# A two-layer hybrid encoder on one core: reciprocal roots computed as exp(−½·ln) on ScalarE

## The chip, the cores and the metric

The kernel runs on one core of a Trainium2 chip, as one launch. The metric is the time of one execution on the device, in microseconds; the profile adds the span, from the first to the last instruction of a profiled execution. A core has TensorE (PE), VectorE (DVE), ScalarE (ACT), GpSimd (POOL) and SyncE (SP), each with its own in-order queue of instructions, and 16 DMA engines.

## The reference, cut to what matters

256 tokens of 1024 features pass two layers, all in f32. A layer mixes tokens in three branches, sums them through an output projection, and then adds a feed-forward part (PEER) that gathers rows from two tables of experts, chosen by scores. Seven places of a layer divide by a root:

```
h  = x * rsqrt(mean(x*x) + 1e-6)                     # input norm
q, k = q * rsqrt(mean(q*q) + 1e-6), k * ...          # attention, 16 norms per token
o  = o * rsqrt(mean(o*o) + 1e-6)                     # attention output, per head
out = out * rsqrt(mean(out*out) + 1e-6)              # state-space branch
kk = kk / max(sqrt(sum(kk*kk)), 1e-12)               # RWKV branch, per head
y  = (y - mean) * rsqrt(var + 64e-5)                 # RWKV branch, output norm
f  = x * rsqrt(mean(x*x) + 1e-6)                     # input of the feed-forward part
```

The feed-forward part takes 128 experts per token (8 heads of 16): it gathers a row of table u for each, multiplies it with the token's normed features, applies a gelu, weighs it, gathers the expert's row of table v, and sums those rows by weight.

## The kernel before, in words

The work is cut in four units of 128 tokens: layer 0 with tokens 0 to 127 and 128 to 255, then layer 1 with the same. A unit has a mixing (the three branches and the output projection), a choosing of experts (`peer`, `chosen`), and a gather of 256 rows of 128 x 1024 f32, 128 of table u and 128 of table v. POOL issues one indirect DMA per row (L614) into a ring of 15 buffers (`arena`). A row of table u is multiplied with the features on DVE (L1804, L1806); a row of table v is added either on PE (L2393, L2394), by a diagonal matrix of the weights that ACT writes (L1038, four rows ahead, eight diagonals in a ring), or on DVE (L1813, L1817). A buffer is free for the next row once DVE or PE is done with it, and POOL waits for that.

The mixing of unit 0 runs by itself, before there is any expert to gather. From then on the gather of unit n and the mixing and choosing of unit n+1 run beside each other. Every engine has them in one fixed order: the table `ROWS_BY` says, for each named step of the next unit, how many rows of the present one come before it. An engine that waits in a step therefore also holds back the rows that stand behind the step in its queue. The last unit's gather has no mixing beside it.

Each root is taken in the same way: PE or DVE sums the squares, ACT takes the root with the scale and the small constant built in (`x_length` L800, `kk_length` L722, `qk_lengths` L728, `s5_root` L753, `o_roots` L795, `deviation` L857, and in `peer` L993), and DVE inverts it (L1387, L1340 and L1341, L1434, L1284, L1376, L1532, L1698) and multiplies. ACT goes on only when its own result is written. In unit 0 (`first`) the order is written out by hand; in later units the steps `scale`, `gelu`, `abkr`, `saa`, `vara` and `fT` hold them.

ACT evaluates its functions from a table that holds a set of them. Nothing in the kernel's source loads a table: the loads (ACT_TABLE_LOAD in the profile) are put in when the program is built, each in front of an instruction whose function the loaded set lacks. The profile names the line of that instruction, not the set. Copy and Square never have one in front of them here. In `first` three small instructions are there to have a table loaded early: a Sqrt (L862), a Tanh (L878) and an Exp (L882), each on one column.

Of the kernel before, what the change touches and what calls it, by code (L numbers as in the profile page):

```python
# [18 lines left out]
ALU = mybir.AluOpType  # L19
# [3 lines left out]
P = 128  # L23
D_MODEL = 1024
# [179 lines left out]
def build_program(nc, A, out):  # L204
    ctx = ExitStack()
    with ctx:  # L206
        def sb(name, shape, dt=F32):
            return ctx.enter_context(nc.sbuf_tensor(name, shape, dt))
# [47 lines left out]
        small = sb("small", [P, 64])  # L256
        eps = sb("eps", [P, 2])
        cum = sb("cum", [P, 2, P + 1])
# [153 lines left out]

        f_sd, f_r, f_g, f_h, fT_ps, fT_a, fT_v = (sem(i) for i in ("f_sd", "f_r", "f_g", "f_h", "fT_ps", "fT_a", "fT_v"))
        x_half = sem("x_half")
# [161 lines left out]
        def _(pool):  # L576
            own = Chain(s_pool, pool)

            own.add(nc.gpsimd.memset(eps[:, 0:1], NORM_EPS))
            own.add(nc.gpsimd.memset(eps[:, 1:2], RW_EPS))  # L580
            own.add(nc.gpsimd.iota(ti[:], pattern=[[1, P]], base=0, channel_multiplier=0))
            pool.wait_ge(s_pool, own.count)
# [38 lines left out]
        def _(act):  # L621
# [53 lines left out]
            def mixing(n, layer, t):  # L675
# [43 lines left out]
                def kk_length():  # L719

                    act.wait_ge(lora_ps, n + 1)
                    A_(rw["rk"][:, :, :], quad(3)[:, 2:4, :], ACT.Sqrt).then_inc(kk_sd, 1)  # L722
                    act.wait_ge(kk_sd, n + 1)

                def qk_lengths():

                    act.wait_ge(qk_ss, n + 1)
                    A_(small_m[:, 32:48], small_m[:, 16:32], ACT.Sqrt, bias=eps[:, 0:1], scale=1.0 / HD).then_inc(qk_sd, 1)  # L728
                    act.wait_ge(qk_sd, n + 1)
# [20 lines left out]
                def s5_root():  # L750

                    act.wait_ge(gss_ps, n + 1)
                    A_(glu_t[:, 0, :], bank[s5b][:, 0:P], ACT.Sqrt, bias=eps[:, 0:1], scale=1.0 / 256).then_inc(gss_sd, 1)  # L753
                    act.wait_ge(gss_sd, n + 1)
# [37 lines left out]
                def o_roots():  # L792

                    act.wait_ge(oss_ps, n + 1)
                    A_(normed[:, n % 2, 512:1024], bank[4][:, :], ACT.Sqrt, bias=eps[:, 0:1], scale=1.0 / P).then_inc(oss_sd, 1)  # L795
                    act.wait_ge(oss_sd, n + 1)

                def x_length():

                    A_(small_m[:, 1:2], small_m[:, 0:1], ACT.Sqrt, bias=eps[:, 0:1], scale=1.0 / D_MODEL).then_inc(x_sd, 1)  # L800
                    act.wait_ge(x_sd, n + 1)
# [52 lines left out]
                def deviation():  # L854

                    act.wait_ge(var_ps, n + 1)
                    A_(rw["ep"][:, :, :], quad(1)[:, 0:2, :], ACT.Sqrt, bias=eps[:, 1:2], scale=1.0 / HD).then_inc(var_sd, 1)  # L857
                    act.wait_ge(var_sd, n + 1)

                def first():  # L860

                    own(A_(small_a[:, 30:31], eps[:, 0:1], ACT.Sqrt))  # L862
                    act.wait_ge(st_ss, 1)
# [110 lines left out]
            def peer(n, layer, t):  # L974
# [17 lines left out]
                own(A_(work[:, 0:D_MODEL], x[:, t, :], ACT.Square, accum_out=small_p[:, 0:1]))  # L992
                A_(small_p[:, 1:2], small_p[:, 0:1], ACT.Sqrt, bias=eps[:, 0:1], scale=1.0 / D_MODEL).then_inc(f_sd, 1)  # L993
                act.wait_ge(f_sd, n + 1)
# [4 lines left out]
                for g, heads in enumerate(TOP):  # L999
                    yield f"s{g}"  # L1000
                    chunk_used(act, n, Q_NAMES[heads[-1] | 1 if n else heads[-1]])
                    b0 = 2 * heads[0] % 4
                    A_(q_cm[:, 2 * heads[0]:2 * heads[-1] + 2, :], bank_all[:, b0:b0 + 2 * len(heads), 0:P] if n else quad(g % 2)[:, 0:2 * len(heads), :],
                       ACT.Copy).then_inc(pq_ok, 1)
                    act.wait_ge(pq_ok, NT * n + g + 1)
                    act.wait_ge(ps_ps, NT * n + g + 1)
                    if g == 0:
                        act.wait_ge(f_r, n + 1)
                    A_(scores[:, 2 * heads[0]:2 * heads[-1] + 2, :], score_bank(n, g)[:, 0:2 * len(heads), :], ACT.Copy,
                       scale=small_p[:, 2:3]).then_inc(ps_ok, 1)  # L1010
                    act.wait_ge(ps_ok, NT * n + g + 1)
                    if n == 0 and g == 0:
                        normed_copied(0)
# [54 lines left out]
        def _(dve):  # L1068
# [139 lines left out]
            def mixing(n, layer, t):  # L1208
# [72 lines left out]
                def s5_normed():  # L1281

                    dve.wait_ge(gss_sd, n + 1)
                    own(V.reciprocal(glu_t[:, 0, :], glu_t[:, 0, :]))  # L1284
                    for hf in range(2):
# [51 lines left out]
                def products():  # L1337

                    dve.wait_ge(kk_sd, n + 1)
                    own(ts(rw["rk"][:, :, :], rw["rk"][:, :, :], 1e-12, None, ALU.max))  # L1340
                    own(V.reciprocal(rw["rk"][:, :, :], rw["rk"][:, :, :]))  # L1341
                    own(tt(rw["kk"][:, :, :], rw["kk"][:, :, :], rw["rk"][:, :, :], ALU.mult))
                    dve.wait_ge(exps, n + 1)
# [28 lines left out]

                def o_scale():

                    dve.wait_ge(oss_sd, n + 1)
                    own(V.reciprocal(normed[:, n % 2, 512:1024], normed[:, n % 2, 512:1024]))  # L1376

                def attended():

                    stt(mixed[:, 0:4, :].rearrange("p a t -> p (a t)"), bank[3][:, :], subln[:, layer:layer + 1],  # L1380
                        normed[:, n % 2, 512:1024], ALU.mult, ALU.mult).then_inc(mix_d, 1)
                    dve.wait_ge(mix_d, n + 1)

                def scaled():

                    dve.wait_ge(x_sd, n + 1)
                    own(V.reciprocal(small_m[:, 2:3], small_m[:, 1:2]))  # L1387
                    ts(normed[:, n % 2, :], x[:, t, :], small_m[:, 2:3], None, ALU.mult).then_inc(h_ok, 1)
                    dve.wait_ge(h_ok, n + 1)
# [41 lines left out]
                def qk_normed():  # L1431

                    dve.wait_ge(qk_sd, n + 1)
                    own(V.reciprocal(small_m[:, 32:48], small_m[:, 32:48]))  # L1434
                    for i in range(2):
# [93 lines left out]
                def gated():  # L1529

                    dve.wait_ge(var_sd, n + 1)
                    own(V.reciprocal(rw["ep"][:, :, :], rw["ep"][:, :, :]))  # L1532
                    own(tt(rw["y"][:, :, :], rw["y"][:, :, :], rw["ep"][:, :, :], ALU.mult))
# [7 lines left out]
                def first():  # L1541
# [49 lines left out]
                    right_side()  # L1591
                    o_scale()
                    attended()
# [7 lines left out]
                def beside_rows():  # L1601
# [57 lines left out]
                    yield "y"  # L1659
                    o_scale()  # L1660
                    attended()
# [30 lines left out]
            def peer(n, layer, t):  # L1692
# [4 lines left out]
                dve.wait_ge(f_sd, n + 1)  # L1697
                V.reciprocal(small_p[:, 2:3], small_p[:, 1:2]).then_inc(f_r, 1)  # L1698
                dve.wait_ge(f_r, n + 1)
                ts(normed[:, n % 2, :], normed[:, n % 2, :], small_p[:, 2:3], None, ALU.mult).then_inc(f_h, 1)  # L1700
# [734 lines left out]
```

## Time and profile before

| | |
|---|---|
| time, median of three runs | 1849.23 us (1845.07 to 1852.96) |
| profiled execution, span | 1836.8 us |
| profiled execution, own time outside the span | not recorded |
| DVE busy | 1418.5 us, 77% |
| ACT busy | 383.6 us, 21% |
| POOL busy | 1133.0 us, 62% |
| PE busy | 1366.3 us, 74% |
| HBM traffic | 638.65 MB read, 348 GB/s over the span |
| ACT_TABLE_LOAD | 73, of 1283 ns each |

An engine's busy time is an average over stages with different limits. In the rows below a timeline row begins with the start and the duration in us; the bracket at its end is the idle time of the engine just ahead of it and what ended that. "issue" means that the profile shows nothing that it waited for. A DMA share near 1 says that all 16 DMA engines are busy.

### The profile page before, as it was taken

Reading aid. Unit: us, or ns where it says so; the run is one execution under the profiler, and the core shown is the slowest. Engines: PE = TensorE matmul, PEld = TensorE weight load, DVE = VectorE, ACT = ScalarE, POOL = GpSimd, SP = SyncE. Lnnn points to the kernel's source line nnn. Section 1 sums busy time; section 2 is a strip of 40 time slices with the busy share of each in tenths; the row PEclk is TensorE's granted clock in tenths of the full one; section 3 lists DMA queues with packets and bytes.
Section 4 is the critical chain, followed back from the end, with each engine's and each line's share of the span. In section 5 each row is a group of like instructions: output and inputs, shape, how many; then the busy total and the mean of one; then the engine's idle time right before and its main releaser. Section 6 shows DMA issues by size and latency. Waiting matters only on the chain. (4 is left out here: it accounts for less than half of the span.)

```text
span 1836.8 us, 17575 instructions
## 1 busy us (share of the span) xinstructions
PE 1366.3 (74%) x5274; PEld 783.4 (43%) x5274; DVE 1418.5 (77%) x3427; ACT 383.6 (21%) x933; POOL 1133.0 (62%) x1046
## 2 busy tenths in 40 slices
PE   7889498687978388867888777967978837555557
PEld 6567354255456144334455363434546413222122
DVE  7867699997679669898668799887867875576653
ACT  2332221322111121322121221311221212001000
POOL 2002576777674756477657787576677766666664
PEclk9979699989899689989899989988999958978989
DMA  7348998999999998998999999999999999999998
GB/s 222 127 146 285 337 367 336 409 367 357 373 401 395 331 371 310 338 352 321 387 386 404 403 393 407 338 346 346 364 381 405 386 392 348 357 354 354 371 367 323
DMA packets 204723, 640.90 MB, mean 349 GB/s; under 512 B 18603, under 2 KB 35861, under 8 KB 204629
## 3 DMA queue, kind: packets, MB, share of 16 engines
q0 software_dynamic: 147920, 538.25, 77.0%
q1 hardware_dynamic: 56172, 100.96, 15.6%
q8 instruction: 43, 0.70, 0.2%
q10 hardware_dynamic: 536, 0.57, 0.1%
q14 instruction: 52, 0.42, 0.1%
HBM read 638.65 MB, written 1.05 MB: 348 GB/s over the span
## 5 line engine op out<-in xcount | busy, mean ns | idle before, releaser
L614 POOL DMA_INDIRECT arena<-in_peer_u_dram,expert x512 | 563.6, 1101 | 416.8 <-DVE expert L1768 150.3
L614 POOL DMA_INDIRECT arena<-in_peer_v_dram,expert x512 | 559.7, 1093 | 264.8 <-issue 152.4
L2393 PE MATMUL bank<-arena,diag 128*128 128x512 f32 x768 | 443.1, 660 | 269.2 <-DMA arena<-in_peer_v_dram,expert 122.2
L1806 DVE SCALAR_TENSOR_TENSOR arena<-arena,normed 128x1024 f32<-128x1024 f32 x364 | 434.1, 1224 | 70.5 <-DMA arena<-in_peer_u_dram,expert 53.7
L2394 PE MATMUL bank<-arena,diag 128*128 128x512 f32 x768 | 426.6, 637 | 7.3 <-issue 6.9
L2393 PEld LDWEIGHTS bank<-arena,diag 128*128 128x128 f32 x768 | 141.0, 205 | 474.4 <-issue 408.2
L2394 PEld LDWEIGHTS bank<-arena,diag 128*128 128x128 f32 x768 | 158.3, 206 | 213.9 <-issue 213.9
L1804 DVE SCALAR_TENSOR_TENSOR arena<-arena,bank 128x1024 f32<-128x1024 f32 x148 | 175.7, 1219 | 77.5 <-DMA arena<-in_peer_u_dram,expert 46.5
L1038 ACT ACTIVATE diag<-ident,weight 128x128 f32<-128x128 f32 x384 | 128.6, 391 | 235.6 <-DVE weight L1823 101.2
L1881 PE MATMUL bank<-h_cm,wring 128*128 128x128 f32 x1152 | 150.0, 291 | 32.0 <-issue 20.2
L1881 PEld LDWEIGHTS bank<-h_cm,wring 128*128 128x128 f32 x1152 | 146.1, 207 | 45.6 <-issue 37.5
L1817 DVE SCALAR_TENSOR_TENSOR x<-arena,weight,x 128x1024 f32<-128x1024 f32 x96 | 123.4, 1286 | 16.3 <-DMA arena<-in_peer_v_dram,expert 12.7
L1897 PE MATMUL bank<-wring,h_cm 128*128 128x512 f32 x192 | 91.7, 627 | 12.4 <-DMA wring<-in_w_in_dram 11.8
L1042 ACT ACTIVATE dots<-dots 128x16 f32<-128x16 f32 x32 | 6.9, 216 | 350.2 <-DVE arena L1806 146.2
L1897 PEld LDWEIGHTS bank<-wring,h_cm 128*128 128x128 f32 x192 | 38.0, 203 | 59.0 <-issue 42.9
L1905 PE MATMUL bank<-wring,h_cm 128*128 128x512 f32 x128 | 61.7, 632 | 1.1 <-DVE h_cm L1538 1.1
L1813 DVE SCALAR_TENSOR_TENSOR bank<-arena,weight,bank 128x1024 f32<-128x1024 f32 x30 | 38.6, 1288 | 18.5 <-DMA arena<-in_peer_v_dram,expert 11.4
L2092 PE MATMUL bank<-work 128*128 128x128 f32 x192 | 31.8, 317 | 23.1 <-DVE work L1494 11.2
L836 ACT ACTIVATE work<-bank 128x512 f32<-128x512 f32 x24 | 14.3, 595 | 165.1 <-PE bank L2092 102.0
L2092 PEld LDWEIGHTS bank<-work 128*128 128x128 f32 x192 | 28.2, 221 | 36.5 <-DVE work L1494 16.6
L1763 DVE SCALAR_TENSOR_TENSOR work<-work 128x64 f32<-128x64 f32 (+1 forms) x320 | 41.3, 205 | 1.9 <-issue 1.2
L1042 ACT ACT_TABLE_LOAD x24 | 30.8, 1283 | 56.4 <-issue 26.3
(443 smaller groups left out, 1573.3 us busy)
## 6 DMA issues: line engine op xcount, KB each, us to landing
wring<-in_w_in_dram SPq DMA_DIRECT2D x40, 1024.0 KB
wring<-in_peer_w_q_dram SPq DMA_DIRECT2D x25, 1024.0 KB
wring<-in_w_out_dram SPq DMA_DIRECT2D x16, 1024.0 KB
arena<-in_peer_u_dram,expert POOLq DMA_INDIRECT x512
arena<-in_peer_v_dram,expert POOLq DMA_INDIRECT x512
arena<-in_peer_w_q_dram SPq DMA_DIRECT2D x7, 1024.0 KB, 10.7
wring<-in_w_in_dram SPq DMA_DIRECT2D x4, 512.0 KB
x<-in_x_dram SPq DMA_DIRECT2D x2, 512.0 KB, 5.6
```

The source lines that it names most:

```text
L614: nc.gpsimd.indirect_dma_start(out=rows[g % RING], out_offset=None, in_=tables[kind], in_offset=bass.IndirectOffsetOnAxis(ap=expert[:, n % ...
L1038: A_(diag[:, p % DIAGS, :], ident[:, :], ACT.Copy, scale=weight[:, slot:slot + 1]).then_inc(s_diag, 1)
L1763: own.add(stt(picks[c // 8][:, c % 8, :].rearrange("p (a b) -> p a b", b=TOPK), places, float(c), ids, ALU.is_equal, ALU.mult))
L1804: ins = stt(row2, row2, 1.0, hb_psum[n], ALU.mult, ALU.mult, accum_out=dots[:, slot:slot + 1])
L1806: ins = stt(row, row, 1.0, hb, ALU.mult, ALU.mult, accum_out=dots[:, slot:slot + 1])
L1817: ins = stt(x[:, t, :], row, weight[:, slot:slot + 1], x[:, t, :], ALU.mult, ALU.add)
L1881: last = mm(bank[b0 + j][:, 0:P], w[:, k, P * j:P * j + P], source[:, 4 * part + k, :], start=part == 0 and k == 0, stop=part == 1 and k == 3)
L1897: last = mm(bank[b0][:, :], h_cm[:, 4 * part + k, :], w[:, k, :], start=part == 0 and k == 0, stop=part == 1 and k == 3)
L1905: last = mm(bank[4 + half_][:, :], mixed[:, OUT_K[name] + k, :], w[:, k, 512 * half_:512 * half_ + 512], start=name == "out0" and k == 0, ...
L2092: last = mm(quad(0)[:, i, :], ms[k % 2][:, i, :], inv[:, i, :], start=True, stop=True)
L2393: mm(bank[6][:, :], d, row[:, 0:512], start=first, stop=end)
L2394: mm(bank[7][:, :], d, row[:, 512:1024], start=first, stop=end).then_inc(s_pe_used, 1)
```

## The change

All seven roots become a logarithm and an exponential, both on ACT: ln(scale·x + constant), then exp(−½ · that). The result is the reciprocal root itself, so DVE's reciprocals go. For `kk_length` a constant 1e-30 is put under the logarithm, and the clamp, the reciprocal and the product (L1340 to L1342) become one DVE instruction. ACT waits for the logarithm to be written before the exponential. The semaphore f_r goes: ACT's scores are scaled by its own result. The early Sqrt of L862 becomes an early Ln; the early Tanh and Exp stay.

```diff
-        eps = sb("eps", [P, 2])
+        eps = sb("eps", [P, 3])
...
+            own.add(nc.gpsimd.memset(eps[:, 2:3], 1e-30))
...
                 def kk_length():
                     act.wait_ge(lora_ps, n + 1)
-                    A_(rw["rk"][:, :, :], quad(3)[:, 2:4, :], ACT.Sqrt).then_inc(kk_sd, 1)
+                    own(A_(rw["rk"][:, :, :], quad(3)[:, 2:4, :], ACT.Ln, bias=eps[:, 2:3]))
+                    A_(rw["rk"][:, :, :], rw["rk"][:, :, :], ACT.Exp, scale=-0.5).then_inc(kk_sd, 1)
...
                 def qk_lengths():
-                    A_(small_m[:, 32:48], small_m[:, 16:32], ACT.Sqrt, bias=eps[:, 0:1], scale=1.0 / HD).then_inc(qk_sd, 1)
+                    own(A_(small_m[:, 16:32], small_m[:, 16:32], ACT.Ln, bias=eps[:, 0:1], scale=1.0 / HD))
+                    A_(small_m[:, 32:48], small_m[:, 16:32], ACT.Exp, scale=-0.5).then_inc(qk_sd, 1)
...
                 def o_roots():
-                    A_(normed[:, n % 2, 512:1024], bank[4][:, :], ACT.Sqrt, bias=eps[:, 0:1], scale=1.0 / P).then_inc(oss_sd, 1)
+                    own(A_(normed[:, n % 2, 512:1024], bank[4][:, :], ACT.Ln, bias=eps[:, 0:1], scale=1.0 / P))
+                    A_(normed[:, n % 2, 512:1024], normed[:, n % 2, 512:1024], ACT.Exp, scale=-0.5).then_inc(oss_sd, 1)
...
                 def first():
-                    own(A_(small_a[:, 30:31], eps[:, 0:1], ACT.Sqrt))
+                    own(A_(small_a[:, 30:31], eps[:, 0:1], ACT.Ln))
...
                     act.wait_ge(ps_ps, NT * n + g + 1)
-                    if g == 0:
-                        act.wait_ge(f_r, n + 1)
...
                 def products():
                     dve.wait_ge(kk_sd, n + 1)
-                    own(ts(rw["rk"][:, :, :], rw["rk"][:, :, :], 1e-12, None, ALU.max))
-                    own(V.reciprocal(rw["rk"][:, :, :], rw["rk"][:, :, :]))
-                    own(tt(rw["kk"][:, :, :], rw["kk"][:, :, :], rw["rk"][:, :, :], ALU.mult))
+                    own(stt(rw["kk"][:, :, :], rw["rk"][:, :, :], 1e12, rw["kk"][:, :, :], ALU.min, ALU.mult))
...
-                def o_scale():
+                def attended():
                     dve.wait_ge(oss_sd, n + 1)
-                    own(V.reciprocal(normed[:, n % 2, 512:1024], normed[:, n % 2, 512:1024]))
...
                 dve.wait_ge(f_sd, n + 1)
-                V.reciprocal(small_p[:, 2:3], small_p[:, 1:2]).then_inc(f_r, 1)
-                dve.wait_ge(f_r, n + 1)
```

`x_length`, `s5_root`, `deviation` and the root in `peer` are changed like `qk_lengths`, and the DVE reciprocals of L1284, L1387, L1434 and L1532 are taken out.

## Rows read from the trace of the kernel before

**Rows 1.** The profile's page, part 1: busy us, share of the span and instructions of each engine.
```profile
PE 1366.3 (74%) x5274; PEld 783.4 (43%) x5274; DVE 1418.5 (77%) x3427; ACT 383.6 (21%) x933; POOL 1133.0 (62%) x1046
```

**Rows 2.** Windows: us, busy of each engine, granted clock, DMA share, GB/s.
```profile
300.00:400.00 100.00, 77.99 (x273) 39.74 (x274) 96.14 (x181) 28.18 (x63) 77.89 (x67) 0.90 1.02 399
...
720.00:830.00 110.00, 85.00 (x300) 43.44 (x300) 96.57 (x210) 28.65 (x66) 72.20 (x65) 0.89 0.94 345
```

**Rows 3.** Waits of POOL: who waited for whom, us in total, times, longest.
```profile
POOL arena L614 <- DVE expert L1768: 150.3, 2, 147.9
...
POOL arena L614 <- PE bank L2394: 108.9, 45, 13.5
...
POOL arena L614 <- DVE arena L1806: 62.2, 14, 10.7
```

**Rows 4.** Lines view of DVE, shapes apart: xcount, busy us, mean ns, idle before.
```profile
L1376 DVE RECIPROCAL normed<-normed 128x512 f32<-128x512 f32 x4 | 13.4, 3353 | 15.9 <-issue 9.7 <-ACT normed L795 6.2
...
L1341 DVE RECIPROCAL rw_rk<-rw_rk 128x256 f32<-128x256 f32 x4 | 7.0, 1754 | 0.1
...
L1532 DVE RECIPROCAL rw_ep<-rw_ep 128x256 f32<-128x256 f32 x4 | 7.0, 1752 | 5.1 <-ACT rw_ep L857 5.1
...
L1284 DVE RECIPROCAL work<-work 128x128 f32<-128x128 f32 x3 | 2.9, 953 | 0.1
```

**Rows 5.** Timeline of ACT, 10 to 157 us: start, us, line, operation, idle before.
```profile
10.33 0.29 ACT L800 ACTIVATE small_m<-small_m,eps 128x1 f32<-128x1 f32 x1 [4.53 <-DVE normed L1545]
...
54.34 0.20 ACT L693 ACTIVATE small_m<-eps 128x1 f32<-128x1 f32 x1
...
123.09 0.69 ACT L795 ACTIVATE normed<-bank,eps 128x512 f32<-128x512 f32 x1
...
123.81 0.38 ACT L851 ACTIVATE work<-bank 128x256 f32<-128x256 f32 x1
...
128.77 1.28 ACT L740 ACT_TABLE_LOAD   x1 [4.58 <-DVE arena L1266]
...
131.79 0.37 ACT L746 ACTIVATE arena<-bank,half 128x128 f32<-128x128 f32 x1 [1.31 <-PE bank L1945]
...
140.93 0.47 ACT L857 ACTIVATE rw_ep<-bank,eps 128x256 f32<-128x256 f32 x1 [3.61 <-PE bank L2143]
...
152.74 0.30 ACT L993 ACTIVATE small_p<-small_p,eps 128x1 f32<-128x1 f32 x1
...
156.03 0.38 ACT L1003 ACTIVATE work<-bank 128x256 f32<-128x256 f32 x1 [1.73 <-PE bank L1872]
```

**Rows 6.** Timeline of ACT in the second mixing, 347 to 354 us.
```profile
347.43 0.31 ACT L728 ACTIVATE small_m<-small_m,eps 128x16 f32<-128x16 f32 x1
...
348.19 1.28 ACT L746 ACT_TABLE_LOAD   x1
...
353.99 1.28 ACT L1042 ACT_TABLE_LOAD   x1
```

**Rows 7.** Timeline of DVE, 54 to 142 us.
```profile
54.68 0.16 DVE L1188 TENSOR_TENSOR neg_lam<-small 128x1 f32<-128x1 f32 x1
...
123.91 3.35 DVE L1376 RECIPROCAL normed<-normed 128x512 f32<-128x512 f32 x1 [6.24 <-ACT normed L795]
...
141.53 1.75 DVE L1532 RECIPROCAL rw_ep<-rw_ep 128x256 f32<-128x256 f32 x1 [1.47 <-ACT rw_ep L857]
```

**Rows 8.** Timeline of DVE in the second mixing, at 347 us.
```profile
347.77 0.25 DVE L1434 RECIPROCAL small_m<-small_m 128x16 f32<-128x16 f32 x1
```

**Rows 9.** Timeline of PE, 124 to 146 us.
```profile
124.89 0.43 PE L2126 MATMUL bank<-rw_rp,state 64*64 64x128 f32 x2
...
130.53 1.16 PE L1945 MATMUL bank<-arena,glu_w 128*128 128x128 f32 x8 [0.89 <-ACT arena L740]
...
145.36 3.70 PE L1905 MATMUL bank<-wring,h_cm 128*128 128x512 f32 x8 [1.10 <-DVE h_cm L1538]
```

**Rows 10.** Timeline of DVE in the third mixing, at 916 us.
```profile
916.42 1.75 DVE L1532 RECIPROCAL rw_ep<-rw_ep 128x256 f32<-128x256 f32 x1 [3.60 <-ACT rw_ep L857]
```

More of the change, by code:

```diff
@@ L411, in build_program @@
         x_mid = sem("x_mid")
-        f_sd, f_r, f_g, f_h, fT_ps, fT_a, fT_v = (sem(i) for i in ("f_sd", "f_r", "f_g", "f_h", "fT_ps", "fT_a", "fT_v"))
+        f_sd, f_g, f_h, fT_ps, fT_a, fT_v = (sem(i) for i in ("f_sd", "f_g", "f_h", "fT_ps", "fT_a", "fT_v"))
         x_half = sem("x_half")
@@ L752, in s5_root @@
                     act.wait_ge(gss_ps, n + 1)
-                    A_(glu_t[:, 0, :], bank[s5b][:, 0:P], ACT.Sqrt, bias=eps[:, 0:1], scale=1.0 / 256).then_inc(gss_sd, 1)
+                    own(A_(glu_t[:, 0, :], bank[s5b][:, 0:P], ACT.Ln, bias=eps[:, 0:1], scale=1.0 / 256))
+                    A_(glu_t[:, 0, :], glu_t[:, 0, :], ACT.Exp, scale=-0.5).then_inc(gss_sd, 1)
                     act.wait_ge(gss_sd, n + 1)
@@ L794, in o_roots @@
                     act.wait_ge(oss_ps, n + 1)
-                    A_(normed[:, n % 2, 512:1024], bank[4][:, :], ACT.Sqrt, bias=eps[:, 0:1], scale=1.0 / P).then_inc(oss_sd, 1)
+                    own(A_(normed[:, n % 2, 512:1024], bank[4][:, :], ACT.Ln, bias=eps[:, 0:1], scale=1.0 / P))
+                    A_(normed[:, n % 2, 512:1024], normed[:, n % 2, 512:1024], ACT.Exp, scale=-0.5).then_inc(oss_sd, 1)
                     act.wait_ge(oss_sd, n + 1)
                 def x_length():
-                    A_(small_m[:, 1:2], small_m[:, 0:1], ACT.Sqrt, bias=eps[:, 0:1], scale=1.0 / D_MODEL).then_inc(x_sd, 1)
+                    own(A_(small_m[:, 1:2], small_m[:, 0:1], ACT.Ln, bias=eps[:, 0:1], scale=1.0 / D_MODEL))
+                    A_(small_m[:, 2:3], small_m[:, 1:2], ACT.Exp, scale=-0.5).then_inc(x_sd, 1)
                     act.wait_ge(x_sd, n + 1)
@@ L856, in deviation @@
                     act.wait_ge(var_ps, n + 1)
-                    A_(rw["ep"][:, :, :], quad(1)[:, 0:2, :], ACT.Sqrt, bias=eps[:, 1:2], scale=1.0 / HD).then_inc(var_sd, 1)
+                    own(A_(rw["ep"][:, :, :], quad(1)[:, 0:2, :], ACT.Ln, bias=eps[:, 1:2], scale=1.0 / HD))
+                    A_(rw["ep"][:, :, :], rw["ep"][:, :, :], ACT.Exp, scale=-0.5).then_inc(var_sd, 1)
                     act.wait_ge(var_sd, n + 1)
                 def first():
-                    own(A_(small_a[:, 30:31], eps[:, 0:1], ACT.Sqrt))
+                    own(A_(small_a[:, 30:31], eps[:, 0:1], ACT.Ln))
                     act.wait_ge(st_ss, 1)
@@ L992, in peer @@
                 own(A_(work[:, 0:D_MODEL], x[:, t, :], ACT.Square, accum_out=small_p[:, 0:1]))
-                A_(small_p[:, 1:2], small_p[:, 0:1], ACT.Sqrt, bias=eps[:, 0:1], scale=1.0 / D_MODEL).then_inc(f_sd, 1)
+                own(A_(small_p[:, 1:2], small_p[:, 0:1], ACT.Ln, bias=eps[:, 0:1], scale=1.0 / D_MODEL))
+                A_(small_p[:, 2:3], small_p[:, 1:2], ACT.Exp, scale=-0.5).then_inc(f_sd, 1)
                 act.wait_ge(f_sd, n + 1)
@@ L1283, in s5_normed @@
                     dve.wait_ge(gss_sd, n + 1)
-                    own(V.reciprocal(glu_t[:, 0, :], glu_t[:, 0, :]))
                     for hf in range(2):
@@ L1371, in turned_k @@
                     dve.wait_ge(kT_ok, n + 1)
-                def o_scale():
+                def attended():
                     dve.wait_ge(oss_sd, n + 1)
-                    own(V.reciprocal(normed[:, n % 2, 512:1024], normed[:, n % 2, 512:1024]))
-                def attended():
                     stt(mixed[:, 0:4, :].rearrange("p a t -> p (a t)"), bank[3][:, :], subln[:, layer:layer + 1],
@@ L1386, in scaled @@
                     dve.wait_ge(x_sd, n + 1)
-                    own(V.reciprocal(small_m[:, 2:3], small_m[:, 1:2]))
                     ts(normed[:, n % 2, :], x[:, t, :], small_m[:, 2:3], None, ALU.mult).then_inc(h_ok, 1)
@@ L1433, in qk_normed @@
                     dve.wait_ge(qk_sd, n + 1)
-                    own(V.reciprocal(small_m[:, 32:48], small_m[:, 32:48]))
                     for i in range(2):
@@ L1531, in gated @@
                     dve.wait_ge(var_sd, n + 1)
-                    own(V.reciprocal(rw["ep"][:, :, :], rw["ep"][:, :, :]))
                     own(tt(rw["y"][:, :, :], rw["y"][:, :, :], rw["ep"][:, :, :], ALU.mult))
@@ L1591, in first @@
                     right_side()
-                    o_scale()
                     attended()
@@ L1659, in beside_rows @@
                     yield "y"
-                    o_scale()
                     attended()
```

## The prediction

> **What bounds the kernel now.** I read the page first. DVE is the busiest engine, PE next, and ACT has the most room, with 383.6 us of 1836.8 [rows 1]: that invites the change. Then the waits of POOL: it issues no gather until DVE has the first experts, a wait of 147.9 us [rows 3]. Up to there the kernel is one chain of DVE, ACT and PE, and what the chain gains or loses there should move everything behind it. Then the windows. From 300 to 400 us the 16 DMA engines are full (share 1.02, 399 GB/s) while DVE is busy for 96.14 of 100 us; from 720 to 830 us the share is 0.94 and DVE is busy for 96.57 of 110 us [rows 2]. So the gathers are bound by transfers in some stretches, and in others they lose a few per cent because buffers come free late: POOL waits 108.9 us for PE and 62.2 us for DVE's products to free a row [rows 3]. Relief on DVE is worth something there, but not its full size. Unit 3's gather has no root beside it and should not change.
>
> **What is taken off DVE.** Per unit it is 3.35 us (attention output), 1.75 (kk), 1.75 (variance) and 0.95 (state space) [rows 4], the clamp of kk (an estimate of 0.3, between nothing and the 0.38 us that ACT takes for the same 128x256 [rows 5]), and three small reciprocals, of which one took 0.25 [rows 8]; I count 0.57 for the three. That is 8.7 us, and 34.7 us for four units. The product of kk is replaced by an instruction of the same shape and two inputs, so it costs the same.
>
> **What is put on ACT.** 28 exponentials. By shape they should cost what the roots cost: 0.69 us for 128x512 from PSUM with a bias [rows 5], down to 0.30 for a column. Without a bias I take 0.60 for the largest; about 12 us for all. The price that decides is another. A table load takes 1.28 us, and it comes each time the loaded set lacks the function [rows 5]. How will Ln and Exp be placed? The trace shows two things on this. At 128.77 a load precedes the Gelu, and the Tanh at 131.79 has none in front of it: one set holds both [rows 5]. Yet at 348.19 a load is made for a Tanh, and at 353.99 another for the Gelu that follows [rows 6]. A placement that looked ahead would have taken the common set once. So each function gets its own usual set, whatever follows. I therefore expect a load for Ln and then another for Exp at every root, unless Ln's usual set happens to hold Exp too.
>
> The Trainium skill says otherwise. "ScalarE activation tables: per-element evaluation and per-set limits", section "Table sets in the compiler and the runtime", says that loads are placed greedily for the longest run, and "ScalarE: Activation LUTs", section "Table sets: the hidden batching unit", gives ln followed by exp one load, since a set holds both. By that rule this is rival 1. The trace agrees with the pages' 1283 ns for a load [rows 5] and speaks against the longest run [rows 6].
>
> I walked along ACT's order of functions in the trace with the rule "the usual set of the function, when the loaded one lacks it"; it gives the 73 loads of the trace, each at its line. With Ln and Exp in the roots' place, and in different sets, it gives 101: 56 at the roots (two each, but one at the first `x_length`, whose Ln was loaded early, and none saved elsewhere at a root), fewer at the exponentials and Tanh that follow. So 28 loads more, 35.9 us of ACT. With one set for both it gives 65.
>
> **Unit 0, step by step** (two loads per root).
> - `x_length`. The root at 10.33 takes 0.29 us [rows 5] and DVE waits for it. Now: Ln, load 1.28, Exp 0.30, less the small reciprocal 0.16 and its gap: +1.4 us. Everything behind waits for h, so all of it stays.
> - kk. DVE is 2.1 us sooner done, but next waits for the decays, whose last ACT instruction starts at 54.34 for 0.20 us; DVE went on at 54.68 [rows 5, 7]. Gain 0.1: call it 0. ACT's +2.9 fits ahead of the decays, where the early Exp no longer needs a load.
> - qk. DVE comes to it 5 us after ACT is done, and PE is behind its projection then: 0.
> - Attention output. Root 123.09 to 123.78, reciprocal 123.91 to 127.26 [rows 5, 7]. Now the Exp ends at 123.78 + 1.28 + 0.60 = 125.7: DVE has the result 1.6 us sooner. But ACT's next, the solved rows of RWKV (L851) at 123.81, starts at 125.7, and PE's outputs that wait for it move from 124.89 [rows 9] to 126.1. Behind them PE had idled 0.89 us for the Gelu at 130.53 [rows 9]; the Gelu now comes early, so this idle time goes, and the gated part is late by 0.3.
> - Variance. The root starts at 140.93 after a wait for PE and has no load [rows 5]; now the loaded set is Exp's. 141.2 + load 1.28 + Ln 0.47 + load 1.28 + Exp 0.38 = 144.6, against 141.53 + 1.75 = 143.3 [rows 7]. PE's last output projection waits for this at 145.36 [rows 9]: +1.4 in all.
> - Feed-forward. The root at 152.74 has no load before it; two come, and an Exp: +2.9, of which ACT's idle 1.73 us before 156.03 [rows 5] hides the most: +1.1 for the scores and the first experts.
>
> The sum of the terms is 1.4 + 1.4 + 1.1 = +4 us until the first gather. Its bounds are +2 (the loads of variance and feed-forward placed in a wait) and +6.
>
> **Units 1 to 3.** DVE is relieved of 8.7 us in each, but of the attention output's 3.35 only 1.5 count, since it waits for ACT there: 6.9 each, 20.6 in all. Against this stand new waits. kk and qk follow each other on ACT and grow together by 3 loads and two exponentials, 4.5 us; in unit 1 DVE took the qk root at 347.77, at once after ACT's 347.43 + 0.31 [rows 6, 8]. There and in unit 3 all 4.5 are a wait, in unit 2 some 2.2. Behind the waiting instruction stand DVE's rows. The feed-forward root adds 2.3 and 1.4 in two units, and the variance, for which DVE waited 3.60 us in unit 2 [rows 10], gives its 1.7 back there. That makes 16.6 us of waits. Net: −4 us of DVE's time, of which between none and two thirds passes to the end (the windows with a share below 0.97 are some two thirds of the stretch): −1.5. ACT's other instructions, above all the diagonals that PE waits for, come 1.3 to 4.5 us later behind each root; I give that +1.5, from 0 to +12. So 0, from −4 to +12.
>
> **Sum.** +4 on 1836.8. The time of the profiled execution outside its span isn't given; the median of the runs is 12.4 us above the span, and I add the difference to the median: 1849.2 + 4 = 1853 us.
>
> **Rival 1, one set for both.** Unit 0: the first root +0.1; the attention output 2.9 sooner, L851 late by 0.6 which PE's 124.89 hides; gated part −0.9; variance −1.35 more, cut to −2.0 in all by PE's own matmuls: −1.9. Units 1 to 3: 22.5 us of DVE relief, four tenths of it passing: −9. Time 1838 us. For it: a set could hold both. Against it stand the two loads at 348 and 354 us [rows 6].
>
> **Rival 2, slower.** The place is the kk-and-qk pair and the feed-forward root in units 1 to 3, while DVE waits for ACT with rows behind it. The price is the 16.6 us of waits in full, with the relief lost in full transfers: 4 + 16.6 = +21, so 1870 us. It decides if the ring runs full during each wait. For it: DVE is near 90% busy there and can't catch up [rows 2]. Against: 15 buffers cover more than one wait of 4.5 us.
>
> **Rival 3, all relief passes.** If DVE's queue sets the pace wherever the mixing runs, and the waits fall on rows that were late anyway: 4 − 20.6 = −17, so 1832 us. Against it: the DMA share of 1.02 [rows 2].
>
> **Chances.** My forecast 0.62 (own range 1844 to 1863), rival 1 0.14, rival 2 0.15, rival 3 0.07. What can be told from no change is 0.5%, 9 us: below 1840 or above 1858. Faster: half of rival 1, rival 3, and 0.06 of mine, 0.20. Slower: rival 2 and 0.09 of mine, 0.24. Same: 0.56. The range from 1836 to 1868 leaves out most of rivals 2 and 3.
>
> **What would show it.** ACT_TABLE_LOAD 101 times (65: rival 1). A load between every Ln and Exp. The first gather at 172 us instead of 168. DVE busy some 35 us less, ACT some 48 more. DVE idle for ACT at the qk product in units 1 and 3, 4 us or more. The window 300 to 400 with an unchanged DMA share. It is wrong if the first gather comes earlier, or if the shift at the first gather isn't found again at the end.

## The result and the profile after the change

The changed kernel takes 1870.8 us in the median of 4 runs, the kernel before 1849.7 us in 4 runs beside it: ratio 1.0125, 95% interval 1.0085 to 1.0166, 21 us slower. Three later comparisons, each with its own runs of before, gave 1.0073, 1.0063 and 1.0088. I predicted 1853 us (a ratio of 1.002), with a range up to 1868 us. The first measurement is outside it, and for slower I had given 0.24. The ratios leave out runs more than 1.5% above the fastest of their kernel; the only ones are four of the twelve of e9 and two of before beside e9 to e12.

Part 1 of the page of the changed kernel, answering to [rows 1]:

```profile
span 1865.6 us, 17600 instructions
## 1 busy us (share of the span) xinstructions
PE 1383.0 (74%) x5274; PEld 796.1 (43%) x5274; DVE 1385.1 (74%) x3395; ACT 430.1 (23%) x989; POOL 1134.5 (61%) x1047
```

DVE is busy for 33.4 us less and ACT for 46.5 us more; I had forecast 35 and 48. ACT_TABLE_LOAD comes 101 times. Yet the span is 28.8 us longer. That overstates the loss: in all later profiled executions the time is 1.8 or 1.9 us above the span, so that of before took some 1839 us (an estimate), 6 us less than the quickest of its four timed runs. The windows that answer to [rows 2]:

```profile
300.00:400.00 100.00, 75.64 (x263) 37.71 (x262) 92.35 (x179) 30.08 (x62) 75.40 (x62) 0.92 0.95 364
720.00:830.00 110.00, 87.30 (x277) 42.53 (x276) 98.32 (x221) 34.46 (x74) 68.02 (x58) 0.91 0.94 340
```

From 300 to 400 us the DMA share fell from 1.02 to 0.95. This fall isn't found again: from 310 to 410 us the same execution has 1.00, and the window from 300 to 400 us has 1.01 in a later execution of before (e5) and 1.00 to 1.01 in the later ones of the changed kernel (e6, e13, e17). The first place where time is lost is in the timeline of ACT (kk root, then qk root, in unit 1), against [rows 6], and in that of DVE, against [rows 8]:

```profile
357.72 1.28 ACT L723 ACT_TABLE_LOAD   x1
359.02 0.47 ACT L723 ACTIVATE rw_rk<-bank,eps 128x256 f32<-128x256 f32 x1
359.51 1.28 ACT L724 ACT_TABLE_LOAD   x1
360.80 0.42 ACT L724 ACTIVATE rw_rk<-rw_rk 128x256 f32<-128x256 f32 x1
361.24 1.28 ACT L730 ACT_TABLE_LOAD   x1
362.53 0.31 ACT L730 ACTIVATE small_m<-small_m,eps 128x16 f32<-128x16 f32 x1
362.86 1.28 ACT L731 ACT_TABLE_LOAD   x1
364.15 0.22 ACT L731 ACTIVATE small_m<-small_m 128x16 f32<-128x16 f32 x1
```

```profile
364.40 1.29 DVE L1434 TENSOR_TENSOR work<-bank,small_m 128x512 f32<-128x512 f32 x2 [4.57 <-ACT small_m L731]
800.57 1.29 DVE L1434 TENSOR_TENSOR work<-bank,small_m 128x512 f32<-128x512 f32 x2 [2.98 <-ACT small_m L731]
1208.29 1.29 DVE L1434 TENSOR_TENSOR work<-bank,small_m 128x512 f32<-128x512 f32 x2 [4.57 <-ACT small_m L731]
```

Each of the four functions brings its own load, and DVE idles 4.57, 2.98 and 4.57 us for the last (4.5, 2.2 and 4.5 were forecast). The second place is unit 0. The expert indices of the first gather are written at 179.40 us, not at 167.61 us: 11.8 us later, where I had forecast 4. At 109 us, ahead of the attention output's root, this pair of traces is already 4.6 us apart, of which the first root made 1.3 (a later pair, e5 and e6, is 0.9 apart there). The timeline of PE behind that root, against [rows 9]:

```profile
127.83 1.96 PE L1927 MATMUL bank<-arena,cT 128*32 128x128 f32 x32
130.77 0.69 PE L2118 MATMUL bank<-rw_rp,state 64*64 64x128 f32 x2 [0.99 <-ACT work L857]
132.86 0.69 PE L2118 MATMUL bank<-rw_rp,state 64*64 64x128 f32 x2
134.94 0.69 PE L2118 MATMUL bank<-rw_rp,state 64*64 64x128 f32 x2
137.03 0.69 PE L2118 MATMUL bank<-rw_rp,state 64*64 64x128 f32 x2
139.12 2.08 PE L1937 MATMUL bank<-arena,glu_w 128*128 128x128 f32 x8
```

PE idles 0.99 us for the solved rows, which stand behind the attention output's root on ACT. Its matmuls then take 0.69 us where [rows 9] have 0.43, and the four groups of outputs 8.35 us where they took 5.64 with an idle of 0.89 in them. The granted clock is 0.50 (1.2 GHz) from 125 to 140 us; before the change it was 1.00 there.

### The profile page after: what moved, and what is told of

Its sections match the earlier page's. It is cut to its first block and busy times, and to the rows that moved or that the text cites. A ratio compares the mean times of both kernels' runs of the same rounds, so it can differ in the third digit from the quotient of the medians.

```text
span 1865.6 us, 17600 instructions
## 1 busy us (share of the span) xinstructions
PE 1383.0 (74%) x5274; PEld 796.1 (43%) x5274; DVE 1385.1 (74%) x3395; ACT 430.1 (23%) x989; POOL 1134.5 (61%) x1047
## 3 DMA queue, kind: packets, MB, share of 16 engines
HBM read 638.65 MB, written 1.05 MB: 343 GB/s over the span
## 5 line engine op out<-in xcount | busy, mean ns | idle before, releaser
L2084 PE MATMUL bank<-work 128*128 128x128 f32 x192 | 31.3, 314 | 30.4 <-DVE work L1491 23.2
L2092 PE MATMUL bank<-work 128*128 128x128 f32 x160 | 37.0, 318 | 22.0 <-issue 19.1
L1490 DVE TENSOR_TENSOR work<-work,bank 128x512 f32<-128x512 f32 x20 | 13.7, 686 | 45.8 <-PE bank L2093 31.4
```

Source lines behind the costliest of these rows:

```text
L2084: last = mm(quad(0)[:, i, :], ms[k % 2][:, i, :], inv[:, i, :], start=True, stop=True)
```

## Experiments

The kernel before took 1741 to 1744 us beside most of the kernels, and 1847 and 1850 us beside e9 to e12 and in the first measurement (one and the same chip gave 1741 and 1847 us), so each kernel is compared by its ratio to the runs of before beside it. 0.001 is 1.7 us. Edits are against the changed kernel unless said. "First gather" is the time at which the first expert indices are written, from the profiled execution.

| run | loads | ratio (95%) | before | first gather |
|---|---|---|---|---|
| e1_joint | 72 | 0.9997 (0.9982-1.0011) | 1742.8 | 170.8 |
| e2_pad | 101 | 1.0086 (1.0067-1.0105) | 1742.8 | 180.8 |
| e3_unit0 | 80 | 1.0033 (1.0019-1.0048) | 1742.8 | 174.6 |
| e4_later | 95 | 1.0026 (1.0015-1.0037) | 1742.8 | 168.9 |
| e5_before | 73 | one run, 1738.6 us | 1741.3 | 170.9 |
| e6_after | 101 | 1.0073 (1.0055-1.0092) | 1741.3 | 179.1 |
| e7_solved | 101 | 1.0052 (1.0034-1.0069) | 1741.3 | 173.9 |
| e8_joint_solved | 72 | 1.0002 (0.9988-1.0015) | 1741.3 | 170.3 |
| e9_fill | 101 | 1.0049 (1.0007-1.0091) | 1846.9 | 176.9 |
| e10_kq | 95 | 1.0035 (1.0004-1.0067) | 1846.9 | 179.4 |
| e11_rest | 86 | 1.0091 (1.0058-1.0125) | 1846.9 | 174.5 |
| e12_early | 68 | 0.9999 (0.9962-1.0037) | 1846.9 | 169.7 |
| e13_after | 101 | 1.0063 (1.0041-1.0086) | 1742.2 | 174.6 |
| e14_kq | 95 | 1.0035 (1.0021-1.0049) | 1742.2 | 177.6 |
| e15_fill | 101 | 1.0069 (1.0045-1.0092) | 1742.2 | 175.0 |
| e16_kq_fill | 95 | 1.0029 (1.0016-1.0042) | 1742.2 | 176.2 |
| e17_after | 101 | 1.0088 (1.0074-1.0102) | 1744.0 | 178.6 |
| e18_early | 68 | 0.9999 (0.9988-1.0010) | 1744.0 | 169.5 |

### Loads and relief apart (e1, e2)

e1_joint, ahead of the early Ln and of the Ln of 23 of the roots:

```
+ nc.scalar.add_instruction(mybir.InstLoadActFuncSet(..., act_func_set_id=6, ...))
  own(A_(tmp, in_, ACT.Ln, ...))
  A_(inv, tmp, ACT.Exp, scale=-0.5).then_inc(done, 1)
```

> The changed kernel with one instruction added in front of 25 of the 28 roots: it loads the one table set that holds both Ln and Exp, so that no load comes between them. 72 table loads instead of 101, all else as in the changed kernel. Theory A (the second load of each root is what costs: waits of VectorE for ScalarE in all units, and in unit 0 a stretch of TensorE at half clock behind them): the stretch at half clock from 130 us goes, the first gather comes at 168 to 170 us as before the change instead of 179, VectorE's idle time for ScalarE falls from 84 us to about 45, and the time is that of rival 1 of the prediction, 1838 to 1845 us. Theory B (the extra loads only fill idle time, and the loss comes from ScalarE's exponentials or from gathers that collide otherwise): 1860 to 1870 us, though the loads are gone.

e2_pad, against the kernel before:

```
- A_(sd, in_, ACT.Sqrt, ...).then_inc(done, 1)
+ own(A_(sd, in_, ACT.Sqrt, ...))
+ A_(small_a[:, 29:30], eps[:, 0:1], ACT.Exp).then_inc(done, 1)
```

> The kernel before, with its roots and VectorE's reciprocals, but after each of the 28 roots ScalarE runs an exponential of one column, with the load that this takes, before it signals the root: 101 table loads, as in the changed kernel, and no relief of VectorE. Theory A (loads cost, and the relief of VectorE is worth something in units 1 to 3): slower than the changed kernel, by the reciprocals (8 us in each unit, some of it hidden by transfers): 1880 to 1890 us. Theory B (the gathers are bound by transfers, so relief is worth nothing, and all that counts is the loads): as the changed kernel, 1868 to 1873 us. Theory C (the loads cost little, something else does): 1850 to 1858 us. In unit 0 all theories of loads expect a first gather later than the 179 us of the changed kernel, near 183.

In e1 the set was loaded by hand 24 times (23 roots, not the 25 of the expectation). One table set does hold both functions; only the placement didn't choose it. With it (e1) the loss is gone: 0.9997. With the loads and without the relief (e2) it is 1.0086, beside 1.0063 to 1.0088 for the changed kernel, which has both. So the 28 extra loads account for the whole loss. The 33 us that DVE is relieved of, together with the exponentials that ACT takes over, come to nothing in e1, and to between nothing and 4 us in e2 against the changed kernel (which was timed on other chips than e2). My theory A was right on the loads and wrong on the gain: neither 1838 us nor a gap of 10 us between e2 and the changed kernel came. The waits that are listed for DVE show where the relief went. DVE is busy for 33.7 us less in e1 than in e5, and waits 13.8 us more for ACT (57.5 against 43.7; the changed kernel in e6 has 84.7, and theory A asked for about 45), 23.4 us more for PE (69.2 against 45.8) and 4.2 us more for DMA. So a part of the relief turns into waits for ACT, whose second instruction at each root and remaining loads come later (the sum of the added waits, 41.4 us, is above 33.7, since e1's profiled execution was 7.9 us longer than e5's). A kernel with the relief and without the exponentials was not run, so what the relief alone is worth stays open. The two longest of the waits for PE, e5_before first, then e1_joint (line, what it waited for, us in total, times, longest):

```profile
DVE x L1731 <- PE bank L1953: 10.0, 4, 3.7
DVE work L1541 <- PE bank L2149: 8.3, 5, 2.7
```

```profile
DVE work L1541 <- PE bank L2149: 21.3, 8, 6.7
DVE x L1731 <- PE bank L1953: 15.6, 4, 7.2
```

DVE comes earlier to the level updates of the solve and to the residual sum, and waits there for PE: 36.9 us for these two in e1 against 18.3 us. The windows from 830 to 1100 us in the same two executions (columns as in [rows 2]):

```profile
830.00:1100.00 270.00, 217.86 (x890) 131.50 (x891) 218.61 (x583) 56.72 (x133) 193.80 (x169) 0.93 1.03 399
```

```profile
830.00:1100.00 270.00, 218.94 (x905) 133.45 (x905) 214.06 (x583) 57.88 (x135) 199.41 (x167) 0.93 1.03 400
```

DVE is busy for 4.6 us less, and the same bytes move: here the transfers were full before (1.03), and the relief could not add any.

### The halves (e3, e4)

```
- NEW = {(n, r) for n in range(UNITS) for r in ALL}
+ NEW = {(0, r) for r in ALL}                          (e3_unit0)
+ NEW = {(n, r) for n in range(1, UNITS) for r in ALL} (e4_later)
```

NEW names the units and roots that use Ln and Exp; the others keep root and reciprocal.

> Logarithm and exponential in unit 0 alone; units 1 to 3 keep root and reciprocal. Theory A (the shift at the first gather, 11.8 us in the trace, passes whole to the end, and units 1 to 3 add the rest): first gather at 179 us, time 1859 to 1863 us. Theory B (the gathers take it back later, and the loss is made in units 1 to 3, rival 2 of the prediction): 1850 to 1855 us.

> Logarithm and exponential in units 1 to 3 alone; unit 0 as before the change. Theory A (units 1 to 3 account for what the median lost beyond the shift of the first gather, 21 less 12): first gather at 168 us, time 1856 to 1862 us, and the two halves add up to the whole. Theory B (rival 2: waits of VectorE for ScalarE in units 1 to 3 pass whole, and unit 0 counts for little): 1865 to 1870 us. The forecast of the prediction for this part alone was no change, 1846 to 1861 us.

Unit 0 alone costs 0.0033 (5.7 us), units 1 to 3 alone 0.0026 (4.5 us). Both are under theory A's ranges (for unit 0 the loss lies where theory B had it, at 1 to 6 us), and theory B's 15 to 20 us for units 1 to 3 are excluded. In e3's trace the first gather is 5.7 us later than in e4's, on the same chip, and that is what unit 0 costs in the timed runs: in this pair of executions the shift is found again at the end. The two halves add up to 10 us; the changed kernel's three later measurements are 11, 13 and 15 us, with intervals that begin at 7, 10 and 13 us.

### The same kernels on this chip (e5, e6)

> The kernel before, instruction for instruction, for its trace on the chip of the experiments. All theories: first gather and later milestones as in the run with unit 0 unchanged (first gather within 0.5 us of it), the span near 1740 us.

> The changed kernel, instruction for instruction, timed against the kernel before on the chip of the experiments. Theory A (the two halves add up: 5.1 us for unit 0 alone and 5.3 for units 1 to 3 alone were measured): 10 us slower than before, ratio 1.006. Theory B (the 21 us of the first measurement, ratio 1.0125, hold on every chip, and the halves don't add up): 22 us slower. Where all gathers are as fast as in the last four runs, part of what the first measurement lost would be hidden, which speaks for A.

Theory A's additive 10 us is at the lower edge of e6's interval (9.6 to 16 us); 22 us are excluded here. The first gather of e5 is 3.3 us later than in the first execution of the same program, 2 us later than in e4, whose unit 0 is the same, and not within the 0.5 us expected. TensorE's clock differs there between two executions of the same program. The windows of PE from 70 to 75 us in the first execution of before, in the first of the changed kernel, and in e5 (PE busy, granted clock, DMA share, GB/s):

```profile
70.00:75.00 5.00, 5.00 (x25) 1.00 0.00 0
```

```profile
70.00:75.00 5.00, 4.36 (x21) 0.50 0.00 0
```

```profile
70.00:75.00 5.00, 5.00 (x23) 0.50 0.00 0
```

The first execution of before had 1.00 where the others have 0.50, so a part of the first pair's 11.8 us is not the edit's: e6 against e5 the first gather is 8.1 us later. e6 repeats the picture of PE shown above, 0.98 us of idle and 8.35 us of outputs.

### TensorE's clock in unit 0 (e7, e8, e9, e13, e15)

e7_solved and e8_joint_solved (the latter with e1's loads):

```
-  o_roots()
   solved()
+  o_roots()
   s5_gelu()
```

> The changed kernel with one swap in unit 0: ScalarE writes the solved rows of RWKV, for which TensorE waits, ahead of the root of the attention output and its load, instead of behind them. All 101 loads stay. Theory A (TensorE's wait for the solved rows behind the root, with its matmuls at half clock after it, is a main part of the loss in unit 0): the idle 1 us of TensorE at its first output goes, the stretch at half clock gets shorter, the gated part is 2 to 5 us earlier and the first gather 2 to 4 us earlier than in the changed kernel; the time 2 to 4 us less. Theory B (VectorE's own queue and the loads of variance and feed-forward set unit 0): first gather within 1 us of the changed kernel's, same time.

> The kernel with the one table set for both functions (72 loads) and the same swap in unit 0. Theory A: the swap has less to win here, since only one load and no second one stands in front of the solved rows: first gather 0.5 to 1.5 us earlier than in the kernel with the one set alone, and with it at or ahead of the kernel before; time 1740 to 1743 us against 1742.8 before. Theory B: no difference from the kernel with the one set alone.

e9_fill:

```
- s5_output()
+ s5_output((0, 0, 1))
```

> The changed kernel with all its loads and its order on ScalarE, but in unit 0 TensorE runs the first half of the state-space output twice (16 matmuls more, an estimate of 1.0 us from 1.96 us for 32 of them), so that it has work where it idled 0.98 us for the solved rows. Theory A (the idle at the end of a long stretch at half clock is what keeps the clock down): the outputs start at the same 130.4 us, but after the first group or two they take 1.17 us each and not 2.09, the gated part is 3 to 4 us earlier than in the changed kernel, the first gather 2 to 4 us earlier, the time 2 to 4 us less. Theory B (the clock follows something else, such as the loads or the state of the chip): outputs at half clock to the end as before, first gather and time as in the changed kernel, at most 1 us more.

PE in e7_solved, then in e9_fill:

```profile
128.15 0.69 PE L2174 MATMUL bank<-rw_rp,state 64*64 64x128 f32 x2
130.24 0.69 PE L2174 MATMUL bank<-rw_rp,state 64*64 64x128 f32 x2
132.22 0.43 PE L2174 MATMUL bank<-rw_rp,state 64*64 64x128 f32 x2
133.39 0.43 PE L2174 MATMUL bank<-rw_rp,state 64*64 64x128 f32 x2
```

```profile
128.00 2.81 PE L2000 MATMUL bank<-arena,cT 128*32 128x128 f32 x48
130.94 0.61 PE L2191 MATMUL bank<-rw_rp,state 64*64 64x128 f32 x2
132.30 0.43 PE L2191 MATMUL bank<-rw_rp,state 64*64 64x128 f32 x2
133.47 0.43 PE L2191 MATMUL bank<-rw_rp,state 64*64 64x128 f32 x2
134.64 0.43 PE L2191 MATMUL bank<-rw_rp,state 64*64 64x128 f32 x2
```

Without the idle before the outputs the clock returns during them, whether the idle goes by the swap or by matmuls put in its place while ACT does what it did. In e9 the first gather is 2.2 us earlier than in e6; the interval of its ratio (1.0007 to 1.0091) holds the changed kernel's three later ratios, so its time decides nothing. In e7 the first gather was 5.1 us earlier than in e6, more than theory A's 2 to 4, and the time 3.5 us less by the medians; the two intervals overlap. In e8 the gain over e1 was 0.5 us, as expected. But the same program as e6, in e13:

```profile
126.01 1.40 PE L2000 MATMUL bank<-arena,cT 128*32 128x128 f32 x32
128.95 0.43 PE L2191 MATMUL bank<-rw_rp,state 64*64 64x128 f32 x2 [1.55 <-ACT work L891]
130.12 0.43 PE L2191 MATMUL bank<-rw_rp,state 64*64 64x128 f32 x2
131.29 0.43 PE L2191 MATMUL bank<-rw_rp,state 64*64 64x128 f32 x2
132.46 0.43 PE L2191 MATMUL bank<-rw_rp,state 64*64 64x128 f32 x2
```

Here the clock had risen before the idle, and it stayed. So the long stretch is not a property of the program. In nine executions with the loads in unit 0 and this idle (0.6 to 1.6 us) - the changed kernel four times, e2, e3, e10, e11, e14 -, the outputs up to the next matmul took 8.35, 8.35, 4.68, 8.23, 8.34, 6.62, 8.34, 6.58 and 7.42 us, 7.4 in the mean; in those without it (before, e4, e5, e1, e8, e12, e18) 5.3 to 5.6 us. But e7, with the loads and without the idle, took 6.4 us, about as e3 and e11 with it (6.6): the idle lengthens the stretch on the average, and isn't all that sets it. The repeat beside e13:

> The changed kernel, instruction for instruction, as the mark for the three runs beside it. All theories: 1.007 to 1.0125 of before, as measured twice.

> The changed kernel with TensorE's idle time in unit 0 filled, again, beside the changed kernel. Theory A (3 to 4 us of half clock after that idle pass whole to the end): 0.0015 to 0.003 under the ratio of the changed kernel. Theory B (they are caught up by the gathers): the same ratio within 0.001.

e15's ratio is 1.0069 beside e13's 1.0063: no gain that can be told, though the intervals (0.002 each way) don't exclude theory A's 0.0015 fully. e13 and e15 both had the clock already, with first gathers at 174.6 and 175.0 us, so their traces cannot tell the theories apart; only the timed runs speak: e15's median is 1.0 us below e13's, its ratio 0.0006 above, and this leans to B. In e15 PE idled 1.05 us before the outputs all the same.

### kk and qk, and the other roots (e10, e11, e14, e16)

```
+ load of set 6 ahead of the Ln of kk, n > 0        (e10_kq, e14_kq; e16 with e9's edit too)
+ load of set 6 ahead of the Ln of x, s5, o, var, f, n > 0   (e11_rest)
```

> The changed kernel with the one table set loaded ahead of the kk root in units 1 to 3, so that kk and qk together need one load and not four (95 loads in all). VectorE waits 4.57, 2.98 and 4.57 us for the qk root in the trace of the changed kernel. Theory A (rival 2 of the prediction in small: these waits are what units 1 to 3 lose, 5.3 us): the waits fall to under 1 us each and the time to 4 or 5 us less than the changed kernel, 1.004 to 1.005 of before. Theory B (the waits are absorbed by the ring, the loss comes from the other roots or from rows of ScalarE that TensorE waits for): the waits go but the time stays within 1.5 us of the changed kernel.

> The complement of the last: the one table set loaded ahead of the other five roots in units 1 to 3 (86 loads), kk and qk as in the changed kernel. Theory A (the kk and qk pair costs it): within 1.5 us of the changed kernel. Theory B (attention output, variance and feed-forward cost it, where VectorE waits 3.3 to 6.6 us for one root each): 3 to 5 us less than the changed kernel. If both this and the last gain 2 to 3 us, the loss is spread.

> One set for kk and qk in units 1 to 3, again, beside the changed kernel. Theory A (the waits for this pair are what units 1 to 3 lose): 0.003 or more under the ratio of the changed kernel. Theory B: within 0.0015 of it.

> Both edits in one kernel. Theory A (the two are separate parts of the loss and add up): 0.005 to 0.007 under the ratio of the changed kernel, so 1.002 to 1.006 of before, where what is left is the other loads of unit 0. Theory B: no better than the better of the two alone.

DVE's waits for the qk root, in e13_after and then in e14_kq:

```profile
DVE work L1502 <- ACT small_m L643: 13.4, 3, 4.6
```

```profile
DVE work L1502 <- ACT small_m L643: 1.2, 2, 0.7
```

12.2 us of waits go. The time falls by 0.0028 (e14 against e13) and by 0.0040 (e16 against e15, where the intervals don't touch), 5 to 7 us. That is as much as units 1 to 3 lost in e4, so theory A holds for this pair: about half of its waits passes to the end. For e16's own sum theory A asked 0.005 to 0.007 under e13; it is 0.0034, what the pair gives alone. e11 (1.0091) has a wide interval and no run of the changed kernel beside it; whether the other roots cost something there is left open. e10 gives the same ratio as e14.

### The fewest loads (e12, e17, e18)

e12_early and e18_early are e8 with two edits more:

```
+ load of set 6
  act.wait_ge(var_ps, n + 1)
- load of set 6
  (and no load where the last one was set 6)
```

Of the six loads left out, the one at unit 3's feed-forward root was needed: there the Ln and the Exp each got one again.

> The kernel with the one table set and the swap in unit 0, and besides: its loads stand ahead of ScalarE's waits and not behind them, and six that load what is loaded are left out (68 loads). Against the run with the loads behind the waits, unit 0 has 1.3 us less at the variance and 1.3 us less at the feed-forward root. Theory A (unit 0 passes to the end, as unit 0 alone showed): first gather 2 us earlier than before the change, time 1739 to 1741 where before takes 1742, the fastest of all; theory B (variance and root of unit 0 are covered by TensorE's projections): the same as before, within 1 us.

> The changed kernel, instruction for instruction, once more. Theory A (the loss has one size, 1.006 to 1.007 of before, and the first measurement of 1.0125 was high by its spread of runs): 1.004 to 1.009. Theory B (it is larger where before takes about 1847 us, since the gathers leave less room there): 1.010 or more if this chip is such a one, 1.006 to 1.007 if it is the quicker kind.

> The kernel with 68 loads (one set for both functions, loads ahead of the waits, the swap in unit 0) beside it, once more. Theory A (without the extra loads nothing is lost, and VectorE's relief of 33 us is worth 1 us or nothing): 0.998 to 1.000 of before. Theory B (the relief is worth something once the loads are out of the way): 0.997 or less.

Twice 0.9999: the first gather is 1 us earlier than in e1, and the time is that of before (within 0.1% in e18, 0.4% in e12). Theory A's forecast of 1 to 3 us less than before isn't seen, B's 0.997 in e18 is excluded (interval 0.9988 to 1.0010). No version beats the kernel before. e17 gives 1.0088, at the upper end of theory A's range. The changed kernel's loss is thus 11 to 15 us where before takes 1742 us; the first 1.0125 overlaps these intervals in part, and whether the slower condition makes the loss larger stays open.

## Why the prediction was wrong

**What held.** Two loads at each root and 101 in all; DVE 33.4 us less, ACT 46.5 more; the waits at the qk product; the waits for the feed-forward root (1.87 and 2.43 us in units 1 and 2) and the variance (4.60 us in unit 2, against 3.60 in [rows 10]). In unit 0 the first root's +1.4 was 1.3, the variance's +1.4 (its share from the gated part on) 1.2, the feed-forward's +1.1 was 1.1 (2.6 at its scale, 1.5 of it regained by the experts).

**The step that failed first: "Net: −4 us of DVE's time".** I set 20.6 us of relief against 16.6 us of waits, as if a microsecond of DVE were worth the same wherever it lay. It isn't. A wait stops the queue at one place with rows behind it, and for the pair about half passed (e14, e16). Of the relief nothing passed, net of the exponentials (e1, e8, e12, e18: 0.9997 to 1.0002): from e5 to e1 DVE works 33.7 us less and waits 13.8 us more for ACT, 23.4 for PE and 4.2 for transfers. That the relief came where PE or a transfer was as late as DVE is my reading of these waits; no run has the relief alone. So units 1 to 3 are +4.5 us (e4) and not 0. This is rival 2's mechanism, at a quarter to a third of its 16.6 us. Rival 1 has the same error: one set took the loss away but gave no 11 us.

**The second: "so this idle time goes, and the gated part is late by 0.3".** I put PE's delay behind the solved rows down as a shift, and let the Gelu's idle absorb it. The idle that it makes falls at the end of a stretch at half clock. From e5 to e6 the outputs start 1.9 us later and the next matmul 4.9 us later, where I had 1.7 (the first root's 1.4 and this 0.3). In e13, where the clock was up, the latter is 1.8 us against e4, as forecast, and the first gather is 5.8 us later, in my bounds of +2 to +6. The mean over eight executions with the changed kernel's unit 0 is 177.2 us, over three with the old one 169.1 us: +8.1 us, of which 2 to 3 us are the clock (an estimate, from outputs of 7.3 us against 5.5 in these executions and the matmuls behind them). What unit 0 alone costs in timed runs, 5.7 us, is nearer to what is left without the clock's part, and filling the idle gave nothing that the timed runs could tell.

**The size.** 1853 us stood for +4. By the parts measured it should have been +10, and 1859 us; the whole kernel measures +11 to +15 in three measurements and +21 in the first. My range, to 1868 us, would hold the three, by its width and not by its terms, and misses the first by 3 us. The chance of slower, 0.24, was too low in any case: a net of two opposite terms of 17 and 21 us was given too narrow a range on its bad side. By the bounds of its own terms (+6 and +12) my forecast reaches 1867 us, while its own range stopped at 1863; and the four chances add up to 0.98 only. The 12.4 us that I put between span and median are mostly the spread of runs, since the time outside a span is 1.8 or 1.9 us in the later executions.

## What to carry to other kernels

Price an edit that moves work from a busy engine to an idle one by waits and relief separately: here about half of the wait for one pair of roots passed to the end, and of the relief nothing, net of the exponentials. Look in the trace whether two activation functions in sequence share a load: here Ln and Exp took one each, and the common set loaded by hand turned a loss of 11 to 15 us into none. In a serial start, compare more than one execution before a difference of a few us is put down to the edit.

## What was not expected of the hardware

Loading set 6 by hand serves Ln and Exp but not Tanh, which took its load again (e1, 337.97 us, behind the set's load at 334.72), while the loads stay 1.28 us each. Of e1's 72 loads, seven by hand follow another load of set 6 with none between; the rest are the 65 that I counted for one set. The same program has its stretch of half clock in unit 0 at different places from one execution to the next: 0.50 from 125 to 140 us in e6, and 0.84 and 1.00 in e13. These are the windows of PE from e6 and then e13 (PE busy, granted clock, DMA share, GB/s):

```profile
125.00:130.00 5.00, 4.44 (x42) 0.50 0.46 187
130.00:135.00 5.00, 4.58 (x22) 0.50 0.01 3
```

```profile
125.00:130.00 5.00, 3.45 (x48) 0.84 0.18 75
130.00:135.00 5.00, 5.00 (x43) 1.00 0.01 3
```

And the 105 us between the two levels of before lie in the gathers: from 1470 to 1650 us e5 moves 409 GB/s at a DMA share of 1.03, and the first execution 355 to 370 GB/s at 0.92 to 0.97. What makes the difference isn't shown.
